# Ninety-six seats instead of 128 for each expert of a top-2 mixture of experts

## The reference

```python
logits = (xt @ router).astype(F32)            # xt: 256 x 1024, 8 experts
top_v, top_i = lax.top_k(logits, 2)
gates = jax.nn.softmax(top_v, axis=-1)
dense_gate = jnp.sum(jax.nn.one_hot(top_i, 8, dtype=F32) * gates[..., None], axis=1)
for e in range(8):                            # w1, w3: 1024 x 2816, w2: 2816 x 1024
    h = jax.nn.silu(xt @ w1[e]) * (xt @ w3[e])
    y = y + dense_gate[:, e:e + 1] * (h @ w2[e])
```

## Time and profile before

| | |
|---|---|
| median of 3 runs | 1288.53 us |
| profiled execution | 1288.5 us, its span |
| TensorE matmuls busy | 1247.9 us (97%) |
| VectorE busy | 1052.9 us (82%) |
| ScalarE busy | 837.0 us (65%) |
| mixture of experts | about 522 to 1276 us of the span |
| DMA in the mixture | 383 GB/s over 640 to 1180 us |

### The profile page before, as it was taken

One profiled execution on the slowest core, in us unless ns is written; L12 is line 12 of the kernel. 1 busy time (PEld: TensorE's weight loads), 2 busy tenths in 40 slices (PEclk: granted clock), 3 DMA queues, 4 the chain that ended last, 5 costly groups with the idle time before them and its releaser, 6 DMA issues.

```text
span 1288.5 us, 17344 instructions
## 1 busy us (share of the span) xinstructions
PE 1247.9 (97%) x5932; PEld 1034.4 (80%) x5932; DVE 1052.9 (82%) x1049; ACT 837.0 (65%) x863; POOL 126.5 (10%) x111
## 2 busy tenths in 40 slices
PE   7999999999999979999999999999999999999995
PEld 6889877888878857778888888888888888888884
DVE  5778885455567988889899889888998998898996
ACT  4565654444524474578777777777777777787772
POOL 1063001000004912200000000000000000000001
PEclk9999999999999999999999999999999999999998
DMA  9653058666436515899999999999999999999991
GB/s 351 221 183 104 14 191 294 196 190 210 141 129 209 174 49 197 298 382 384 389 380 387 389 380 387 389 380 387 389 381 382 389 380 381 388 369 376 390 370 53
DMA packets 195058, 374.76 MB, mean 291 GB/s; under 512 B 9392, under 2 KB 27952, under 8 KB 194880
## 3 DMA queue, kind: packets, MB, share of 16 engines
q1 hardware_dynamic: 189072, 351.37, 76.8%
q0 software_dynamic: 5936, 22.74, 4.8%
HBM read 363.07 MB, written 11.01 MB: 290 GB/s over the span
## 4 chain that ended last, share of the span: by engine, by line
PE 90%; DVE 5%; DMA 2%; ACT 1%; issue 1%; POOL 0%; SPq 0%; DVEq 0%; ACTq 0%
PE psum L390 22%; PE psum L392 22%; PE psum L391 22%; PE psum L411 4%; PE psum L412 4%; PE psum L413 4%; PE psum L2040 1%; DMA raw<-in_od_w 1%; DVE wlo L381 1%; PE psum L1572 1%; PE psum L1571 1%; PE psum L1570 1%; PE psum L1712 1%; PE psum L1594 1%; PE psum L1596 1%
## 5 line engine op out<-in xcount | busy, mean ns | idle before, releaser
L381 DVE TENSOR_TENSOR wlo<-raw,whi 128x1536 fp32r<-128x1536 f32 (+1 forms) x426 | 676.6, 1622 | 137.9 <-ACT whi L375 136.8
L375 ACT CAST whi<-raw 128x1536 fp32r<-128x1536 f32 (+1 forms) x426 | 581.8, 1376 | 212.6 <-PE psum L392 176.2
L390 PE MATMUL psum<-whi,xe_hi 128*128 128x512 f32 x704 | 277.8, 395 | 2.8 <-DVE wlo L381 2.5
L392 PE MATMUL psum<-whi,xe_lo 128*128 128x512 f32 x704 | 274.6, 390 | 0.0
L391 PE MATMUL psum<-wlo,xe_hi 128*128 128x512 f32 x704 | 274.1, 389 | 0.0
L390 PEld LDWEIGHTS psum<-whi,xe_hi 128*128 128x128 f32 x704 | 132.2, 188 | 31.2 <-DVE wlo L381 4.2
L392 PEld LDWEIGHTS psum<-whi,xe_lo 128*128 128x128 f32 x704 | 132.1, 188 | 28.1
L391 PEld LDWEIGHTS psum<-wlo,xe_hi 128*128 128x128 f32 x704 | 132.3, 188 | 26.5
L390 PE MATMUL psum<-whi,hTe_hi 128*128 128x512 f32 x352 | 138.4, 393 | 0.0
L392 PE MATMUL psum<-whi,hTe_lo 128*128 128x512 f32 x352 | 137.2, 390 | 0.0
L391 PE MATMUL psum<-wlo,hTe_hi 128*128 128x512 f32 x352 | 137.1, 389 | 0.0
(11 more groups left out here) (333 smaller groups left out, 1482.5 us busy)
## 6 DMA issues: line engine op xcount, KB each, us to landing
raw<-in_od_w SPq DMA_DIRECT2D x262, 768.0 KB, 9.8
raw<-in_od_w SPq DMA_DIRECT2D x95, 512.0 KB, 9.4
raw<-in_ev_w SPq DMA_DIRECT2D x33, 768.0 KB, 4.4
raw<-in_ev_w_in SPq DMA_DIRECT2D x32, 512.0 KB, 6.6
raw<-in_od_w_in SPq DMA_DIRECT2D x24, 512.0 KB, 4.6
raw<-in_od_w SPq DMA_DIRECT2D x32, 384.0 KB, 8.0
raw<-in_ev_w SPq DMA_DIRECT2D x12, 512.0 KB, 3.8
raw<-in_od_w SPq DMA_DIRECT2D x24, 256.0 KB, 7.6
```

The source lines that it names most:

```text
L375: nc.scalar.copy((whi if into is None else into)[i % GT][:, 0:n], src[:, 0:n]).then_inc(hi_done, 1)
L381: nc.vector.tensor_tensor((wlo if into is None else into)[i % GT][:, 0:n], src[:, 0:n], (whi if high is None else high)[i % GT][:, 0:n].bi ...
L390: nc.tensor.matmul(ps, hi, w_h[:, r, :], start=start, stop=False)
L392: ins = nc.tensor.matmul(ps, lo, w_h[:, r, :], start=False, stop=stop)
```

## The change

An expert has 96 seats. The stationary operands of the 396 matmuls are 96 columns wide, their results have 96 partitions, token rows travel and are stored as 96, and the transposes have 96 rows of data and a 96 by 96 identity. The buffers keep their places (every 128 columns) and are used through views of 96. The general rounds become two (rounds 1 and 2, for seats 97 to 192 and 193 to 256), so that every number of tokens still has a seat.

```diff
+CAP = 96
+ROUNDS = -(-S // CAP)
...
+        def seated(tile, k0, kc):
+            return tile[:, k0:k0 + kc, 0:CAP]
+        def seated_bank(bank, kc):
+            return psum[:, bank, 0:kc * P].rearrange("p (k s) -> p k s", s=P)[:, :, 0:CAP]
...
-                pool.dma_start(rows[:], sent[e * P:(e + 1) * P, :]).then_inc(rows_in, 16)
+                pool.dma_start(rows[0:CAP, :], sent[e * CAP:(e + 1) * CAP, :]).then_inc(rows_in, 16)
...
-                pool.dma_start(done_rows[e * P:(e + 1) * P, :], y_out[:]).then_inc(y_sent, 16)
+                pool.dma_start(done_rows[e * CAP:(e + 1) * CAP, :], y_out[0:CAP, :]).then_inc(y_sent, 16)
...
-                nc.scalar.copy(hTe_hi[:, k0:k0 + kc, :].rearrange("p k s -> p (k s)"), psum[:, bank, 0:kc * P]).then_inc(m_thi, 1)
+                nc.scalar.copy(seated(hTe_hi, k0, kc), seated_bank(bank, kc)).then_inc(m_thi, 1)
...
-                nc.vector.tensor_tensor(hTe_lo[:, k0:k0 + kc, :].rearrange("p k s -> p (k s)"), psum[:, bank, 0:kc * P],
-                                        hTe_hi[:, k0:k0 + kc, :].rearrange("p k s -> p (k s)").bitcast(F32),
+                nc.vector.tensor_tensor(seated(hTe_lo, k0, kc), seated_bank(bank, kc), seated(hTe_hi, k0, kc).bitcast(F32),
                                         ALU.subtract).then_inc(m_tlo, 1)
...
-            nc.vector.tensor_scalar(more[:], route[:, TOP, 0, 3:4], float(P), None, ALU.is_gt).then_inc(more_set, 1)
+            nc.vector.tensor_scalar(more[:], route[:, TOP, 0, 3:4], float(CAP), None, ALU.is_gt).then_inc(more_set, 1)
...
-            seats(1)
+            for r in range(1, ROUNDS):
+                seats(r)
...
-                    ins = nc.tensor.matmul(psum[:, 4 + k // 4, (k % 4) * P:(k % 4 + 1) * P],
-                                           xn[:, t, k * P:(k + 1) * P], pick[:, t, :], start=False, stop=(t == NT - 1 and k % 4 == 3))
+                    ins = nc.tensor.matmul(psum[:, 4 + k // 4, (k % 4) * P:(k % 4) * P + CAP],
+                                           xn[:, t, k * P:(k + 1) * P], pick[:, t, 0:CAP], start=False, stop=(t == NT - 1 and k % 4 == 3))
...
-                    ins = nc.tensor.transpose(psum[:, 4 + k // 4, (k % 4) * P:(k % 4 + 1) * P], rows[:, k * P:(k + 1) * P], ident)
+                    ins = nc.tensor.transpose(psum[:, 4 + k // 4, (k % 4) * P:(k % 4) * P + CAP], rows[0:CAP, k * P:(k + 1) * P], ident[0:CAP, 0:CAP])
...
-                    ins = nc.tensor.transpose(psum[:, bank, k * P:(k + 1) * P], h_e[:, (k0 + k) * P:(k0 + k + 1) * P], ident)
+                    ins = nc.tensor.transpose(psum[:, bank, k * P:k * P + CAP], h_e[0:CAP, (k0 + k) * P:(k0 + k + 1) * P], ident[0:CAP, 0:CAP])
...
-                return [[(psum[:, bank, :], xe_hi[:, k, :], xe_lo[:, k, :], k == 0, k == KD - 1)] for k in range(k0, k0 + kc)]
+                return [[(psum[0:CAP, bank, :], xe_hi[:, k, 0:CAP], xe_lo[:, k, 0:CAP], k == 0, k == KD - 1)] for k in range(k0, k0 + kc)]
...
-                return [[(psum[:, 2 * half, :], hTe_hi[:, k, :], hTe_lo[:, k, :], k == 0, k == KF - 1)] for half, k in DN_ROWS[i - N_UP]]
+                return [[(psum[0:CAP, 2 * half, :], hTe_hi[:, k, 0:CAP], hTe_lo[:, k, 0:CAP], k == 0, k == KF - 1)] for half, k in DN_ROWS[i - N_UP]]
```

More of the change, by code:

```diff
@@ L540, in _ @@
             with sp.If(flag):
-                with sp.Fori(0, NE) as e:
-                    load_expert(e + NE, e, range(N_FF))
+                for r in range(1, ROUNDS):
+                    with sp.Fori(0, NE) as e:
+                        load_expert(e + r * NE, e, range(N_FF))
             for t in range(NT):
@@ L943, in block_e @@
                 act.wait_ge(m_h, UB * n + tile0 // N_FF * UB + b + 1)
-                src = psum[:, 2 * (b % 2), 0:NB if b < UB - 1 else NH]
-                nc.scalar.activation(silu_e[:, b % 2, 0:src.shape[1]], src, ACT.Silu).then_inc(m_silu, 1)
+                src = psum[0:CAP, 2 * (b % 2), 0:NB if b < UB - 1 else NH]
+                nc.scalar.activation(silu_e[0:CAP, b % 2, 0:src.shape[1]], src, ACT.Silu).then_inc(m_silu, 1)
                 high_parts(n, [end + GT - 1], last, again)
@@ L982, in _ @@
             with act.If(flag):
-                with act.Fori(NE, 2 * NE) as n:
+                with act.Fori(NE, ROUNDS * NE) as n:
                     high_parts(n, range(GT), True, True)
@@ L1427, in block_e @@
                 dve.wait_ge(m_silu, UB * n + tile0 // N_FF * UB + b + 1)
-                w, src = (NB, psum[:, 2 * (b % 2) + 1, :]) if b < UB - 1 else (NH, psum[:, 2 * (b % 2), NH:2 * NH])
-                nc.vector.tensor_tensor(h_e[:, b * NB:b * NB + w], silu_e[:, b % 2, 0:w], src, ALU.mult).then_inc(m_h, 1)
+                w, src = (NB, psum[0:CAP, 2 * (b % 2) + 1, :]) if b < UB - 1 else (NH, psum[0:CAP, 2 * (b % 2), NH:2 * NH])
+                nc.vector.tensor_tensor(h_e[0:CAP, b * NB:b * NB + w], silu_e[0:CAP, b % 2, 0:w], src, ALU.mult).then_inc(m_h, 1)
                 low_parts(n, [stop + GT - 1], last, end)
@@ L1525, in _ @@
             with dve.If(flag):
[L1526 to L1529, removed]
-                    gather_lo(e + NE)
-                    block_e(e + NE, 0, last=True)
-                    expert(e + NE, e, True)
-                dve.wait_ge(m_acc, 2 * NE + 3)
+                for r in range(1, ROUNDS):
+                    with dve.Fori(0, NE) as e:
+                        low_parts(e + r * NE, range(GT), True)
+                        dve.wait_ge(m_gt, e + (r - 1) * NE + 1)
+                        pick_tokens(e + r * NE, e)
+                        gather_lo(e + r * NE)
+                        block_e(e + r * NE, 0, last=True)
+                        expert(e + r * NE, e, True)
+                dve.wait_ge(m_acc, 2 * (ROUNDS - 1) * NE + 3)
                 for t in range(NT):
@@ L2013, in gather @@
                     for t in range(NT):
-                        ins = nc.tensor.matmul(psum[:, 4 + k // 4, (k % 4) * P:(k % 4 + 1) * P],
-                                               xn[:, t, k * P:(k + 1) * P], pick[:, t, :], start=(t == 0), stop=(t == NT - 1))
+                        ins = nc.tensor.matmul(psum[:, 4 + k // 4, (k % 4) * P:(k % 4) * P + CAP],
+                                               xn[:, t, k * P:(k + 1) * P], pick[:, t, 0:CAP], start=(t == 0), stop=(t == NT - 1))
                     if k % 4 == 3:
@@ L2047, in scatter @@
                     cols = slice(half * NB, (half + 1) * NB)
-                    nc.tensor.matmul(dst, put[:, t * P:(t + 1) * P], y_hi[:, cols], start=True, stop=False)
-                    ins = nc.tensor.matmul(dst, put[:, t * P:(t + 1) * P], y_lo[:, cols], start=False, stop=True)
+                    nc.tensor.matmul(dst, put[0:CAP, t * P:(t + 1) * P], y_hi[0:CAP, cols], start=True, stop=False)
+                    ins = nc.tensor.matmul(dst, put[0:CAP, t * P:(t + 1) * P], y_lo[0:CAP, cols], start=False, stop=True)
                 ins.then_inc(m_sc, 1)
@@ L2113, in _ @@
             with pe.If(flag):
-                with pe.Fori(NE, 2 * NE) as n:
+                with pe.Fori(NE, ROUNDS * NE) as n:
                     pe.wait_ge(m_acc, 2 * n - 2 * NE + 3)
```

44 lines of the change are left out of this document (21 added, 23 removed).

## The result

The changed kernel takes 1296.75 us (median of 5 runs, 1294.3 to 1298.01) against 1288.53 us; the ratio is 1.0056, with an interval of 1.0041 to 1.007. The forecast was 1282.5 us and faster. The profiled execution of the changed kernel has a span of 1295.0 us, 6.5 us more than before's. An execution's time is 1.7 to 1.9 us longer than its span in every record of these kernels. So the traced execution of before (span 1288.5 us) took some 1290.3 us, an estimate, 1.8 us more than its median, while the changed kernel's traced one (1296.75 us) is its median: the two traces show 6.5 of the 8.2 us.

What follows compares the result with a forecast made beforehand. TensorE's matmuls were taken as the bound, with DMA 1 to 1.5% behind. Transposes -6.1, evacuations -0.3 and transfers +0.4 gave -6.0 us from 1288.5: 1282.5 us, range 1273 to 1289.5 us.

Steps and rivals of the forecast that it cites:

- the second part of the sum: The 396 matmuls an expert, 3168 in all: narrowing the stationary operand to 96 columns changes their time by 0.
- 13.3 ns: In each 512-column matmul's 226.7 ns interval, what remains beyond the 213.3 ns stream; taken as a fixed price.
- gain of 10.6 us: Bound for the matmuls if all 13.3 ns scaled with stationary columns: 3.3 ns saved on each of 3168.
- the load's spare time: Before each 512-column matmul, the 188 ns operand load is done 38 ns early, so 96 columns should hide as well.
- Rival (c): Matmul operand loads of 96 columns are slower than of 128, beyond 38 ns of spare: about 1330 us; chance 0.04.
- equal records: Loads of fp32r and float32 operands last 188 and 192 ns, so nothing shows fp32r in a quick form.
- gain nothing: Expert 0's gather matmuls keep a 128-wide load, the bound of 8-column matmuls, so their time stays.
- (a): Rival: transposes get no faster, bound by their 128-wide load at 112 ns; about 1288 us; chance 0.20.
- Rival (d): 96-row transposes between 128-row matmuls switch the array's mode, emptying it at each change: 1298 us; chance 0.04.
- The tight stretch: After 556 us, in early experts where each tile is awaited, TensorE may run into DMA: 0.4 us lost.
- The two limits: TensorE's 93.1 us an expert and DMA's 91.6 us at 389 GB/s; DMA could go 1 to 1.5% faster.
- the transposes' 6.1 us: On TensorE's chain, 228 transposes each save 26.7 ns because 96 identity columns shorten their stream.

Runs made afterwards that it cites:

- three kernels: Changed kernel with one general round, 1292.28 us; kernel before with skipped code written twice, 1293.62 us; changed kernel with general rounds as nested loops, 1292.92 us.
- wide operands: Changed kernel with matmul operands, results and splits 128 wide again; transposes, rows and seats stay 96: 1291.04 us, ratio to before 1.0017.
- the loop in a loop: Changed kernel with both general rounds as one loop in a loop on VectorE and SyncE: 1292.92 us, ratio to before 1.003.
- the kernel with 84 seats: 84 seats instead of 96 in the changed kernel with operands and gather 128 wide and nested general rounds: 1287.51 us, ratio to before 0.9985.

## Why the prediction was wrong

**The step that failed** is the second part of the sum, "I take 0 for this part": the matmuls' 13.3 ns beyond their stream were taken as fixed, and the only bound worked out for them was a gain of 10.6 us. They are 16.7 ns with 96 columns. This adds 0.93 us an expert where TensorE is the bound, and 5.7 us in the runs. The reasoning from the load's spare time was right as far as it went: the load is hidden, and it is 27 ns shorter, 0.84 ns a column. The Trainium skill ("TensorE: Matmul & The Clock Gate", section on LDWEIGHTS) puts a load at its columns over 1.2 GHz, 0.83 ns a column, and the trace agrees with this slope. The interval grew all the same. Rival (c) had the sign and the place, but asked for a load longer than its 38 ns of spare; no such load is in the trace. Full width was the cheapest of the nine widths tried. The Trainium skill's rule on the full 128 (the same page, "Weight-path perf modes") was set aside because of equal records. By its words (a fast load) the record should have grown with 96 columns, and it shrank.

**The general rounds** were costed by whether they run. They don't, but the code that is skipped became longer, and this took some 4 us (4.5, 3.8 and 4.4 us between medians, by three kernels). The sum had no term for it; it wasn't among the rivals either.

**The gather** of expert 0 was costed at nothing by its instructions. The kernel with this part alone is 0.16% slower, 2 us, and runs at half the clock for 8 us or more. The step "gain nothing" looked at the instruction's load and at nothing else; the clock was in no term.

**The transposes** went as said in mechanism: 112 to 82 ns, by their stream, and (a) falls. The size was off: the sum had 0.80 us an expert, and with wide operands it is 0.64, as the load of the next matmul is hidden less. What reached the end was less again (see the transfers). Rival (d) falls too: the first matmul behind a group isn't longer (0.45 us after, 0.48 before), and the kernel that puts transposes of 96 rows between matmuls of 128 is faster than before, by 0.64 us an expert.

**Transfers.** The tight stretch didn't cost the 0.4 us that was added, as TensorE got slower and not faster. The two limits were said to lie 1 to 1.5% apart. With a TensorE 0.7% faster they already met: TensorE stands still for 0.34 and 0.62 us between 556 and 600 us, where the sum had 0.4, and again in the last expert, where it had nothing. Of the transposes' 6.1 us the runs show 1.5 and 2.4, so with every other part at nothing the forecast would still have been some 4 us too low; 1.6 us of this is the last expert's, 1.3 us the smaller size (8 x 0.16), and the rest stays open. The forecast also took before's span (1288.5 us) for its time; spans are 1.8 us shorter, but as only differences were added this didn't move it.

The parts add up in the runs. Taken out of the changed kernel one at a time, the width gives back 0.39% of before's time, the longer code 0.26% (the loop in a loop) and the gather 0.07%: 0.72%, where all three at once give 0.73% and leave 0.17% of gain. Each of these ratios has an interval of about 0.1% to either side; between medians it is 5.7, 3.8 and 2.0 us, 11.5 together, against 10.0. Open is why a narrower operand costs more, and why 120, 80 and 48 columns cost more than 96 and 64. A matmul with fewer stationary columns also writes fewer partitions, and no run tells the two apart.

## What to carry to other kernels

A load that is hidden isn't one that is free: measure the distance from start to start at the new width before narrowing a stationary operand that stands in thousands of matmuls; here 3.3 ns in 227 cost 5.7 us, more than the transposes gave. Cut the small side where it is the stream (the identity of a transpose) and leave the stationary side full. Count the code that is never run: a skipped branch that was unrolled once more cost some 4 us, twice what the transposes gave in the runs, and a loop in a loop took them away again. And where two limits lie 1% apart, a saving on one of them is not worth its full size to the end.

## What was not expected of the hardware

- The interval of fp32r matmuls of 512 columns by stationary width: 226.6 to 227.4 ns at 128, 229.8 to 230.0 at 96, 233.2 to 233.4 at 120, with the load's record at 188 to 190, 161 to 165 and 181 ns.
- VectorE stood 2.60 and 2.23 us without work behind a skipped branch whose code was one round longer, where it had stood 0.29 us and not at all. In the kernel with 84 seats 2.16 us of it came without longer code.
- TensorE's granted clock was at half for 8 us or more with gather matmuls of 96 columns, and at 1.00 from 520 us on with 128, in seven and six profiled executions.
